# Second block of a two-block transformer kernel: stick-breaking and latent attention merged into one list of staggered chains

## The reference, cut to what matters

```
# latent (DSA) attention, 8 heads: each query keeps the 64 best keys by an index score
score = sum_h iw * relu(iq_h . ik);  sel = top_k(score, 64)
o = softmax(q_cat . kv_cat over sel) @ c_kv @ w_uv

# stick-breaking attention, 8 heads
z = q . k;  stay = where(strict, log_sigmoid(-z), 0)
a = where(strict, exp(log_sigmoid(z) + reverse_cumsum(stay) - stay), 0);  o = a @ v

# mLSTM, 4 heads; then the three branches are gated, projected and mixed
mixed = sum_g sigmoid(merge_g) * (branch_g @ w_branch_g);  x = x + mixed @ w_out
```

## Time and profile before

| | us |
|---|---|
| median of 3 executions (lowest, highest) | 1997.39 (1996.8, 2004.06) |
| profiled execution, its own time | 1993.26 |
| its span | 1991.8 |
| PE busy | 1893.2 |
| DVE busy | 1075.1 |
| ACT busy | 871.4 |
| mean granted TensorE clock | 0.985 |

### The profile page before, as it was taken

One profiled execution on the slowest core, in us unless ns is written; L12 is line 12 of the kernel. 1 busy time (PEld: TensorE's weight loads), 2 busy tenths in 40 slices (PEclk: granted clock), 3 DMA queues, 4 the chain that ended last, 5 costly groups with the idle time before them and its releaser, 6 DMA issues. The chain is left out here.

```text
span 1991.8 us, 30805 instructions
## 1 busy us (share of the span) xinstructions
PE 1893.2 (95%) x12540; PEld 1589.3 (80%) x12540; DVE 1075.1 (54%) x2040; ACT 871.4 (44%) x1518; POOL 332.8 (17%) x158
## 2 busy tenths in 40 slices
PE   6999999999999999998999999998999999999996
PEld 3765576777888888686788999987889999789896
DVE  4335655534111111436866656779756776875675
ACT  3313444523322222324555544547564554655453
POOL 0231222343444444230000000110001001000100
PEclk9999999999999999999999999999999999999999
DMA  8332421225222322534226655553434454343441
GB/s 346 124 127 106 143 81 63 75 102 222 96 95 88 106 96 95 203 126 159 86 88 212 208 193 191 179 183 108 143 109 136 138 180 171 105 138 117 134 139 57
DMA packets 76700, 272.28 MB, mean 137 GB/s; under 512 B 8208, under 2 KB 11536, under 8 KB 76560
## 3 DMA queue, kind: packets, MB, share of 16 engines
q1 hardware_dynamic: 74656, 266.37, 38.3%
q10 hardware_dynamic: 1904, 3.94, 0.6%
HBM read 269.23 MB, written 1.05 MB: 136 GB/s over the span
## 5 line engine op out<-in xcount | busy, mean ns | idle before, releaser
L964 PE MATMUL bank<-h,high 128*128 128x256 f32 (+1 forms) x2272 | 741.1, 326 | 20.9 <-issue 4.1
L965 PE MATMUL bank<-h,high 128*128 128x256 f32 (+1 forms) x2272 | 708.8, 312 | 0.0
L966 PE MATMUL bank<-h,low 128*128 128x256 f32 (+1 forms) x2272 | 708.5, 312 | 0.0
L1373 ACT ACTIVATE high<-raw 128x1024 fp32r<-128x1024 f32 x408 | 426.3, 1053 | 211.5 <-PE bank L966 209.2
L964 PEld LDWEIGHTS bank<-h,high 128*128 128x128 f32 x2272 | 432.2, 190 | 103.6 <-issue 56.0
L1770 DVE TENSOR_TENSOR low<-raw,high 128x1024 fp32r<-128x1024 f32 x287 | 357.2, 1249 | 183.3 <-ACT high L1373 181.8
L966 PEld LDWEIGHTS bank<-h,low 128*128 128x128 f32 x2272 | 432.0, 190 | 26.4
L965 PEld LDWEIGHTS bank<-h,high 128*128 128x128 f32 x2272 | 432.3, 190 | 25.7 <-issue 1.7
L1704 POOL TENSOR_TENSOR low<-raw,high 128x1024 fp32r<-128x1024 f32 x121 | 293.8, 2434 | 556.7 <-ACT high L1373 556.7
L1713 POOL TENSOR_TENSOR few<-few,halves 128x2 f32<-128x2 f32 (+2 forms) x27 | 27.0, 998 | 749.6 <-DVE few L1872 749.6
L1814 DVE TENSOR_TENSOR gt<-bank,gt 128x512 f32<-128x512 f32 (+1 forms) x44 | 24.5, 557 | 191.7 <-PE bank L966 189.4
(11 more groups left out here) (292 smaller groups left out, 2710.4 us busy)
## 6 DMA issues: line engine op xcount, KB each, us to landing
raw<-stream SPq DMA_DIRECT2D x504, 512.0 KB, 3.3
xc<-x_in SPq DMA_DIRECT2D x1, 1024.0 KB, 5.4
xc<-ctx_in SPq DMA_DIRECT2D x1, 1024.0 KB, 7.7
out<-xc ACTq DMA_DIRECT2D x1, 1024.0 KB, 4.5
cst<-consts ACTq DMA_DIRECT2D x1, 896.0 KB, 6.5
cst<-consts ACTq DMA_DIRECT2D x1, 704.0 KB, 4.3
ukw<-uk ACTq DMA_DIRECT2D x1, 512.0 KB, 6.4
uvw<-uv ACTq DMA_DIRECT2D x1, 512.0 KB, 7.1
```

The lines of the kernel that those rows point to most:

```text
L964: mm(dst, wh, xh, start=start, stop=False)
L965: mm(dst, wh, xl, start=False, stop=False)
L966: return mm(dst, wl, xh, start=False, stop=stop)
L1373: do(high[:, i % PAIRS, :], raw[:, slot % SLOTS, :], ACTF.Copy).then_inc(S["hi"], 1)
```

## The change

The stick-breaking buffers move out of `prob2` and `tmp` into the part of MG that holds its last gates, which is not yet written then. With that, both attentions are free of each other's buffers, and the two pipelines become one list of eight chains. Each chain has a step, the iteration in which its first pair comes, and a number of blocks. Latent attention begins at iteration 4 (START). In iterations 0 to 3 a chain that has nothing to do gives 3 blocks (LONE), and one pick piece is asked for after every chain (PICKS), active or not, so eight to an iteration.

```
+START, LONE, PICKS = 4, 3, 1

         def stick(p):
             o.step("stick", l, p)
-            o.fill(6)
+            o.fill(4)
             o.step("sticklog", l, p)
-
-        pipeline([stick, lambda p: o.step("stay", l, p), lambda p: o.step("stuck", l, p)], NH // 2, (4, 3, 3), True)
-        o.run(top)
-        o.step("rows", l)
...
...
-        pipeline([two("absorb"), two("latent"), two("turn2"), lambda p: o.step("blend", l, p), lift], NH // 2, (4, 3, 5, 5, 3))
+        chains = ((one("stuck"), 2, 3), (lift, START + 4, 3), (one("blend"), START + 3, 3), (one("stay"), 1, 3),
+                  (two("turn2"), START + 2, 4), (two("latent"), START + 1, 3), (two("absorb"), START, 4), (stick, 0, 4))
+        for i in range(START + 8):
+            for do, begin, blocks in chains:
+                if 0 <= i - begin < NH // 2:
+                    do(i - begin)
+                    o.fill(blocks)
+                elif i < START:
+                    o.fill(LONE)
+                for _ in range(PICKS):
+                    next(top, None)
+            if i == START:
+                o.run(top)
+                o.step("rows", l)
+                o.fill(4)
+                o.step("rowlog", l)
+                o.fill(4)
+                o.step("rowsum", l)
...
+        def stick_of(l, n):
+            return MG[l][:, 12:21, :].rearrange("p j t -> p (j t)")[:, 384 * n:384 * n + 384]
...
-                        b, e = bank_of[step][i], tmp[i]
+                        b, e = bank_of[step][i], stick_of(l, 4 + i)
...
-                        zm = prob2[l][2 * (p % 2) + i]
+                        zm = stick_of(l, 2 * (p % 2) + i)
```

More of the change, by code:

```diff
@@ L544, in second, with pipeline @@
         top = picks()
-        def pipeline(stages, count, fills, picking=False):
+        def pipeline(stages, count, fills):
             depth = len(stages)
@@ L552, in pipeline @@
                     o.fill(fills[s])
-                    if picking:
-                        next(top, None)
         def stick(p):
             o.step("stick", l, p)
-            o.fill(6)
+            o.fill(4)
             o.step("sticklog", l, p)
-        pipeline([stick, lambda p: o.step("stay", l, p), lambda p: o.step("stuck", l, p)], NH // 2, (4, 3, 3), True)
-        o.run(top)
-        o.step("rows", l)
[L564 to L567, removed]
         def two(kind):
@@ L583, in lift, with one @@
                     o.step("gated", l, part)
-        pipeline([two("absorb"), two("latent"), two("turn2"), lambda p: o.step("blend", l, p), lift], NH // 2, (4, 3, 5, 5, 3))
+        def one(kind):
+            return lambda p: o.step(kind, l, p)
+        chains = ((one("stuck"), 2, 3), (lift, START + 4, 3), (one("blend"), START + 3, 3), (one("stay"), 1, 3),
[16 more added lines that the diff above has]
+                o.step("rowsum", l)
         o.step("gcol", l)
@@ L1223, in tensor_program @@
                     pe.wait_ge(*drained["SV", l, 1])
-                    two = [(banks[7][head(i), :], prob2[l][2 * (p % 2) + i], head(2 * p + i)) for i in range(2)]
+                    two = [(banks[7][head(i), :], stick_of(l, 2 * (p % 2) + i), head(2 * p + i)) for i in range(2)]
                     for i, (ps, a, hd) in enumerate(two):
@@ L1587, in scalar_program @@
                         act.wait_ge("stick_abs", at + i)
-                        do(tmp[i][:, 0:384], tmp[i][:, 0:384], ACTF.Exp).then_inc(S["stick_exp"], 1)
+                        do(stick_of(l, 4 + i), stick_of(l, 4 + i), ACTF.Exp).then_inc(S["stick_exp"], 1)
                     for i in range(2):
                         act.wait_ge("stick_exp", at + i)
-                        do(tmp[i][:, 0:384], tmp[i][:, 0:384], ACTF.Ln, bias=1.0).then_inc(S["stick_ln"], 1)
+                        do(stick_of(l, 4 + i), stick_of(l, 4 + i), ACTF.Ln, bias=1.0).then_inc(S["stick_ln"], 1)
                 elif kind == "stay":
@@ L1595, in scalar_program @@
                     for i in range(2):
-                        a = prob2[l][2 * (p % 2) + i]
+                        a = stick_of(l, 2 * (p % 2) + i)
                         act.wait_ge("stayed", 2 * no[step] - 1 + i)
@@ L2111, in vector_program @@
                     for i in range(2):
-                        zm, e = prob2[l][2 * (p % 2) + i], tmp[i]
+                        zm, e = stick_of(l, 2 * (p % 2) + i), stick_of(l, 4 + i)
                         dve.wait_ge("stick", at + i)
```

## The result

The changed kernel took 2020.05 us (median of 4, 2015.07 to 2021.84) beside 1999.2 for the kernel before (median of 4, 1996.8 to 2004.06): ratio 1.0098, interval 1.0076 to 1.0119. It is slower, by about 20 us. I had forecast slower by 10.8 (2008 from 1997.39). The sign held, the size was off by almost a factor of two: 2020.05 lies above the forecast's own range, 2002 to 2017, and just inside the wide one, 1987 to 2021.

The account below looks back on a forecast made before the run. PE was taken to bound the kernel, at DVE's pace in stick-breaking; 2 x (4.4 + 0.0 + 1.0) = 10.8 us on the profiled 1993.26 gave 2004.1, put on the median 1997.39: 2008. Range 2002 to 2017, eight in ten 1987 to 2021.

Parts of the forecast that it names:

- No cost of the buffers, no gain at the end: Moved buffers keep their shapes: 0; the 51 blocks fewer left for the end cost the same there: no gain.
- The front wait of stick-breaking: Stick-breaking: picks ahead of the masks delay DVE; PE waits 11.1 us against 6.7, +4.4 us a layer.
- credit for `rows`: Latent attention: DVE no longer behind when `rows` comes, so two small PE waits go, 1.1 us.
- The two places named: Stick-breaking: the first `stay` waits 2.9 us, the tile of block 64 waits 5 for a copy behind `sticklog`.
- The 2.4 us at the third `stay`: Stick-breaking, second to third `stay`: DVE needs 17.2 us, PE 14.2 and starts 0.7 later, so PE waits 2.4.
- the signs I had named: Profile signs, among them DVE over 90% busy up to the second `sticklog`, first two `stay` waiting at least 4 us together.
- Latent attention: Latent stretch: waits of 2.7 us, 2.3 of them at pair 0's `turn2`, offset by credits; net 0.0, bounds -3.6 to +7.3.
- the credit of 0.9 for the MG copy: Latent stretch: sigmoid pieces fall differently to tiles' ends, so L1404's 1.7 us wait may go; half taken, 0.9.
- Clock: Longer PE waits make half-clock stretches likelier, one or two a layer: 1 us a layer, bounds 0 and 3.4.
- the cover wins: Rival, faster: picks fall into idle DVE time, 17 and 12 blocks hide stick-breaking's chains; -13.4 us, 1984; chance 0.17.
- No change: Rival: front waits cost 4.4 us, the latent side gains its full 3.6; +4 us, 2001; chance 0.25.
- Much slower: Rival: latent attention starves, every pair waits at `turn2`; +27 us, 2025; chance 0.08.

Follow-up runs that it names:

- e1: Kernel before with only the new buffers: its two pipelines and old order kept; ratio 0.9996 to the kernel before.
- e3: Changed kernel with 8 blocks behind `latent` instead of 3 and 6 behind `blend` instead of 3; 1.0140 to the kernel before, median 2029.6 us.
- e6: Changed kernel with 9 blocks behind `absorb` instead of 4; ratio 1.0169 to the kernel before, median 2031.9 us.
- e5: Changed kernel with the four sigmoid pieces and their 16 blocks moved behind the last `lift`; ratio 1.0109 to the kernel before, median 2018.8 us.
- e9: Changed kernel with 12 blocks behind `absorb` instead of 4, eight more per pair; ratio 1.0043 to the kernel before, median 2008.1 us.
- e10: Changed kernel with 6 blocks instead of 4 behind each of `rows` and `rowlog`; ratio 1.0171 to the kernel before, median 2032.6 us.
- e2: Changed kernel with one pick piece after every second chain, four per iteration instead of eight; ratio 1.0044 to the kernel before, median 2007.5 us.
- e7: Changed kernel with six blocks before `sticklog` and two behind, instead of four and four; ratio 1.0069 to the kernel before, median 2012.0 us.
- e11: Changed kernel with the edits of e2, e7 and e9 together; ratio 0.9949 to the kernel before, median 1987.4 us.
- e12: e11 with 8 more blocks behind the last sigmoid piece; ratio 0.9983 to the kernel before.

## Why the prediction was right and wrong

*No cost of the buffers, no gain at the end.* Right for the buffers: e1 is level with before. The end was not tried by itself.

*The front wait of stick-breaking.* Right in mechanism, place and nearly in size. With the credit for `rows` I had 4.4 - 1.1 = 3.3 us a layer and some of the clock; measured were 3.9 and 3.3. The two places named (the first `stay`, the block at the tile behind `sticklog`) wait 3.4 and 3.4, where I had 2.9 and 5.0. The other runs tell why the block waits less: with the same order up to there, it waits 5.2 where no half-clock stretch came between (first layer of e3 and of e6), 4.6 to 4.9 where 3.4 us of it did (e5, e9, e10), and 3.3 to 3.4 behind the changed kernel's 6.8. PE is waiting for DVE and ACT there, and a slow PE only shortens its wait.

But that the sum fits is luck in part. The 2.4 us at the third `stay` (by the prediction's own terms rather 2.3) came neither here nor in the runs with the same order up to there, and of the 1.1 for `rows` a wait of 0.5 is still there (at 1419.5); in their place stands PE's slower work from 1393.9 on, up to 1.7 us.

e2 shows that the picks make the front's loss: half as dense, the stretch is 5.3 us shorter. e7 gives the size of the exposed ACT chain, from one profiled execution each: 1 us with dense picks, and 3.1 beside thinned ones (e11 against e2, the eight blocks more ahead of `latent` counted at 2.8).

Of the signs I had named, two failed: DVE was busy 31.2 of the 36.0 us from the scores to the second `sticklog`, 87% (1356.7 to 1392.8) and not over 90, and the first two `stay` steps waited 3.4 together and not 4, since the rest of the wait fell on the block between them.

*Latent attention.* Here the prediction failed: "Net **0.0**", which with the credit for `rows` taken out is 1.1 us behind the first `latent`, where 4.3 and 6.8 us were lost. Three parts of the step. `turn2` of pair 0 waited 2.8, and its six transposes took 0.3 longer than before (1.12 us against 0.81), where I had 2.3: the bank behind `absorb`'s copy was missing from the working. e6 and e9 show it, since blocks behind `absorb` take this wait away and blocks behind `latent` (e3) do not. The `lift` steps, 0.7 and 1.6 (1.8 in the second layer), were not in the sum at all; I had followed PE's cover for `blend` to `lift` but not what stands before the copy in DVE's queue. And the credit of 0.9 for the MG copy was a guess at the tiles' ends: the whole 1.7 went in both layers, but in the second one of 2.8 came up at another MG copy. One gain I had not seen either: the mLSTM's means (L1094) wait 1.2 us a layer, 2.4 before.

*Clock.* This term failed too: 1 us a layer was too little. Three stretches in the first layer, 13.6 us at half, and four in the second, 17.0, behind waits of 2.8 us and more but for the last, behind 1.8. Taken by kind, the forecast was 8.8 us of waits and 2 of clock for both layers; measured were 8.4 of idle and 9.8 of longer busy time. That the waits add up is luck in part, since `turn2`'s apart those behind the first `latent` stand in other places than forecast. The stretch at 1373.5 costs little, since PE waits for DVE there anyway; those at 1452.0, 1813.8 and 1861.6 are behind `latent`, cost up to 1.7 us each, and make up much of what the three waits leave unexplained. How the loss of a layer splits between a wait and the slow clock behind it was not tried by itself.

*The rivals.* The one on the other side, that the cover wins, failed as the profile had it: DVE was full. But e11 shows that longer cover does win once the picks are spread, 10 us below the kernel before. "No change" named the latent side's gain, and there was none. "Much slower" has the nearest time, but not for its reason: only pair 0 waits at `turn2`.

The table load came out as the earlier trace rows had it: 1.28 us (L1608 at 1371.23, ln at 1372.52), so the drain of which the Trainium skill ("ScalarE: Activation LUTs", What ACT_TABLE_LOAD costs) tells is not seen in this kernel's chain either.

Open: what the loss would be at a full clock, and whether other shifts of the tiles' ends than the few tried here give more.

## What to carry to other kernels

Where every engine follows one written list, cover for a wait is not counted in blocks alone: look at what stands before the step in the queues of ACT and DVE, and whose result that in turn awaits. Filler that comes in tiles has a phase: if other than whole tiles are added or taken between steps, the copies and splits at the tiles' ends fall into other places and can undo what was meant (e6, e10). Whole tiles are the safer step and no safe one: they gained in e9 and lost in e12. Look where each new end falls. Work that nobody waits for yet, as the picks, is to be spread thin over an engine that is full.

## What the runs showed of the hardware

A shift of four blocks, 1.4 us of PE work a layer, moved the whole by 15 us (e10).

TensorE's granted clock fell from 2.4 to 1.2 GHz 70 times in the two layers' stages of the fourteen traces (before, changed, e1 to e12), mostly for 3.4 or 6.8 us, and each time during a wait of PE of at least 1.6 us or within 2.5 us behind its end. It fell at all 27 waits of more than 3.5 us, at 38 of 48 from 2.1 to 3.5, at 5 of 24 from 1.6 to 2.1, and at none of 93 from 0.7 to 1.6. So a wait between 1.6 and 3.5 us did not decide it by itself: at the last `lift`, 1.80 us, the clock fell in the changed kernel's second layer and not in e11, and at the same 2.45 us of the kernel before it fell in the second layer and not in the first. e11, whose waits are at most 1.8 us, has no such stretch in either stage.
